# Attention over paired blocks of queries: which block of a pair goes first, the one of many keys or the one of few

## What is computed

```python
o_a = swa_prompt(qa, ka, va, mk_a, mv_a, attn_sinks, slopes_a)    # window: this chunk of 64 and the two before it, meta keys, a sink
o_b = dsa_prompt(qb, qi, wi, kb, vb, ki, mk_b, mv_b, slopes_b, n_sel_p)  # top 256 of all earlier keys, meta keys
mix = (jax.nn.sigmoid(g_a) * o_a + jax.nn.sigmoid(g_b) * o_b) @ w_o
x = x + rms_norm(mix, g_post_mix)
hid = jnp.square(jax.nn.relu(rms_norm(x, g_pre_mlp) @ w_up))
return x + rms_norm(hid @ w_down, g_post_mlp)
```

## Time and profile before

| what | value |
|---|---|
| median of 3 runs | 1979.54 us (1978.48 to 1980.01) |
| the profiled execution's own time | 1977.99 us |
| its span, first to last instruction | 1976.2 us |
| PE busy | 1888.3 us, 96% |
| DVE busy | 1158.8 us, 59% |
| mean granted clock of PE | 0.982 |
| `attention` on PE | about 582 to 1040 us of the span |

### The profile page before, as it was taken

One profiled execution on the slowest core, in us unless ns is written; L12 is line 12 of the kernel. 1 busy time (PEld: TensorE's weight loads), 2 busy tenths in 40 slices (PEclk: granted clock), 3 DMA queues, 4 the chain that ended last, 5 costly groups with the idle time before them and its releaser, 6 DMA issues. The chain is left out here.

```text
span 1976.2 us, 32638 instructions
## 1 busy us (share of the span) xinstructions
PE 1888.3 (96%) x11780; PEld 1785.9 (90%) x11780; DVE 1158.8 (59%) x2747; ACT 711.8 (36%) x1420; POOL 584.8 (30%) x445
## 2 busy tenths in 40 slices
PE   5999999999999999999997979999999999999995
PEld 5889999877779999999996859999999999999994
DVE  5249999998655666666755653333333333334436
ACT  4335544223334555555653332222222222222212
POOL 2316554234233444444311002222222222222214
PEclk9999999999998999999998989999999999999998
DMA  5423333333446444444204322111111111111204
GB/s 171 126 64 102 95 95 85 89 102 95 115 110 155 98 98 98 98 98 87 67 22 145 117 89 65 48 43 45 45 43 47 45 46 42 42 42 42 64 1 160
DMA packets 180396, 160.23 MB, mean 81 GB/s; under 512 B 101472, under 2 KB 148432, under 8 KB 180288
## 3 DMA queue, kind: packets, MB, share of 16 engines
q1 hardware_dynamic: 166144, 140.32, 25.1%
q10 hardware_dynamic: 14144, 18.49, 4.0%
HBM read 120.63 MB, written 39.27 MB: 81 GB/s over the span
## 5 line engine op out<-in xcount | busy, mean ns | idle before, releaser
L2166 PE MATMUL ps<-x2T_hi,weights 128*128 128x362 f32 (+1 forms) x1536 | 381.5, 328 | 5.3 <-DVE weights L2131 5.3
L2182 PE MATMUL ps<-hid_hi,weights 128*128 128x362 f32 (+1 forms) x1536 | 379.4, 326 | 0.0
L2166 PEld LDWEIGHTS ps<-x2T_hi,weights 128*128 128x128 f32 x1536 | 273.3, 189 | 5.5 <-DVE weights L2131 5.5
L2114 DVE TENSOR_TENSOR total<-total,ps 128x364 f32<-128x364 f32 (+1 forms) x360 | 189.2, 532 | 139.3 <-PE ps L2182 139.3
L2182 PEld LDWEIGHTS ps<-hid_hi,weights 128*128 128x128 f32 x1536 | 270.5, 188 | 0.0
L2166 PE MATMUL ps<-x2T_lo,weights 128*128 128x362 f32 (+1 forms) x768 | 252.4, 329 | 0.0
L2182 PE MATMUL ps<-hid_lo,weights 128*128 128x362 f32 (+1 forms) x768 | 250.2, 326 | 0.0
L976 PE MATMUL ps<-xT_hi,w 128*128 128x362 f32 (+1 forms) x960 | 245.1, 330 | 1.6 <-PEq L160 1.6
L2099 DVE TENSOR_TENSOR hidden<-hidden 128x362 f32<-128x362 f32 (+1 forms) x96 | 51.6, 538 | 311.0 <-ACT hidden L2072 311.0
L2032 POOL TENSOR_TENSOR weights<-down_raw,weights 128x512 fp32r<-128x512 f32 x64 | 83.0, 1296 | 391.7 <-ACT weights L2063 391.7
L951 DVE MATCH_REPLACE8 score<-top,score 128x1024 f32<-128x1024 f32 (+5 forms) x208 | 198.4, 958 | 0.0
(11 more groups left out here) (189 smaller groups left out, 3273.2 us busy)
## 6 DMA issues: line engine op xcount, KB each, us to landing
q_raw<-q_scr SPq DMA_DIRECT2D x80, 256.0 KB, 5.1
w_raw<-in_w_in ACTq DMA_DIRECT2D x64, 256.0 KB, 3.0
up_raw<-in_w_up SPq DMA_DIRECT2D x64, 256.0 KB, 2.7
down_raw<-in_w_down SPq DMA_DIRECT2D x64, 256.0 KB, 2.6
gates<-gate_scr SPq DMA_DIRECT2D x34, 256.0 KB, 4.5
x_in<-in_x_prompt SPq DMA_DIRECT2D x16, 512.0 KB, 4.8
gate_scr<-stage SPq DMA_DIRECT2D x32, 256.0 KB, 3.1
q_scr<-stage SPq DMA_DIRECT2D x40, 181.0 KB, 3.1
```

The source lines that it names most:

```text
L2114: dve.tensor_tensor(out, out, more, ALU.add).then_inc(added, 1)
L2166: last = pe.matmul(ps[:, g % UP_BANKS, 0:n], a[:, k, fs], b, start=(k == 0 and i == 0), stop=(k == KT - 1 and i == 2))
L2182: more = pe.matmul(ps[:, UP_BANKS + g % DOWN_BANKS, 0:n], a[:, f, cols], h, start=(f == 0 and i == 0), stop=(f == FT - 1 and i == 2))
```

## The change

`block_in_pair` gives the block of few keys for e = 0 and that of many for e = 1. All that is addressed by e follows: the order of quads in both branches, the place of a block's queries, its distances, its gates and results. `PAIR_DIST` is written anew, and its value is 1120 columns as before. The pairs, the tiles, the number and the shapes of all instructions are the same.

```diff
     if j == SAMPLE_TILE:
         return SAMPLE_BLOCK
-    return j if e else SAMPLE_BLOCK - 1 - j
+    return SAMPLE_BLOCK - 1 - j if e else j
...
-PAIR_DIST = dist_place(0, 1) + N_META + CHUNK
+PAIR_DIST = dist_place(0, 1) + key_columns(1, block_in_pair(0, 1))
```

## The result

| | median us | runs | ratio to before | 95% interval |
|---|---|---|---|---|
| before | 1979.01 | 18 | | |
| changed | 1982.60 | 18 | 1.0018 | 1.0012 to 1.0025 |

The changed kernel is 3.6 us slower by the medians, 0.18%. That is just within the 0.2% that the forecast called no change, and the interval reaches over it. The profiled execution took 1981.77 us, with a span of 1980.0.

A forecast was written before the change was run, and what follows sets the result against it. PE, busy 96% of the span and gapless through most of the attention, was taken as the bound. +3.5 us from section 1 and -0.3 in tile 1 gave +3.2 on 1979.54, so 1982.7 us; range 1979.7 to 1985.5.

The forecast's parts named there:

- The start of section 1: Tile 0, first score of branch B: PE arrives early and waits 2.4 us for POOL's query split, instead of 0.3.
- The quads from there: Section 1 to tile 1's second quad: S, L, S, L, A1 take 48.5 us against 45.03, so +3.5 us.
- Tiles 1 to 8: Exchanged quad neighbourhoods cost nothing where PE has no gap; -0.3 us in tile 1, 0 elsewhere, within -0.5 to +0.5.
- The split of the loss into 2.1 us of wait and the rest clock: Of the +3.5 us in section 1, 2.1 is the new wait, the rest clock; S loses 2.7 at half clock.
- The clock: Section 1 of tile 0: half clock covers the first S (6.03 us), rising near 613 in the first L (9.40).
- The late clock: Rival, chance 0.25: clock rises one or two steps later in section 1's first L; total +4.6 or +6.0 us.
- The early clock: Rival, chance 0.1: clock rises already in section 1's first S, costing 3.37, with L 8.88; total 0.0, 1979.6 us.
- The third rival: Chance 0.05: DVE sets the pace in tiles 1 to 8 and the order helps; all told -3, 1979.7 us.

The follow-up runs named there:

- e5: Changed kernel with section 0 alone taking its quads in the old order; median 1981.52 us, ratio 1.0007 to the kernel before.
- e3: Changed kernel with POOL's split of section 1's queries done in two halves, each with its own semaphore; median 1978.84 us, ratio 1.0003 to the kernel before.
- e2: Kernel before with the new order in tiles 1 to 7 only, tile 0 in the old order; median 1979.20 us, ratio 1.0004.
- e8: e7 with twenty more wide matmuls inside PE's wait for the first half of POOL's split; median 1975.56 us, ratio 0.9990 to the kernel before.
- e8b: e7b with fourteen more wide matmuls inside PE's wait for the first half of POOL's split; median 1975.65 us, ratio 0.9985 to the kernel before.
- e6r: The same kernel as e6, run again for a second profile; median 1978.29 us, ratio 1.0004 to the kernel before.
- e1: Kernel before with the new order in tile 0 only, the old one in tiles 1 to 7; median 1981.89 us, ratio 1.0017.
- e6: Changed kernel with five matmuls of 512 columns on PE ahead of section 1's wait for POOL; median 1980.10 us, ratio 0.9995 to the kernel before.
- e7: e3 with sixteen wide matmuls in PE's two idle stretches ahead of section 0; median 1978.61 us, ratio 0.9995 to the kernel before.
- e7b: Kernel before, old order, with POOL's split in halves and the wide matmuls of e7; median 1975.98 us, ratio 0.9979.

## Why the prediction was right

Forecast 1982.7, measured 1982.6. That the two lie within 0.1 is luck: the forecast added 3.2 us to a median of 3 runs, 1979.54, and 18 runs have 1979.01, so that the change forecast is +3.2 and the change measured +3.6. And in the profiled executions 0.7 to 0.8 of the difference arises behind the attention, where the forecast had nothing. The attention itself has +3.2 by X and +2.9 by Y. By its steps:

- *The start of section 1.* 2.4 us of waiting for POOL were forecast, 2.27 measured, and the first quad of section 0 took 2.40 us where "no more than the 2.94 us" stood. e5 and e3 took the wait away in two ways, one by work ahead of it and one by an earlier signal, and X fell by 2.2 and 2.6 us.
- *The quads from there.* 6.03, 9.40, 12.02, 8.88, 12.2 were forecast, 6.00, 9.35, 12.01, 8.88, 12.27 measured; +3.5 us in sum, both times. The method carried it: a quad's length depends on what is scored and on what is weighed beside it, and every new neighbourhood but one (A1 behind L) had a twin in the rows of before, and that one was built of two steps that had.
- *Tiles 1 to 8.* -0.3 was forecast for A1 behind a long quad. In the changed kernel A1 behind A14 takes 3.37 us and the lag goes from 3.38 us at 650.65 to 2.98 at the same place of tile 2. From there to the sample tile it stays between 2.96 and 3.23. e2 has the order in these tiles alone and loses nothing.
- *The split of the loss into 2.1 us of wait and the rest clock* is the weak place. The prediction puts 2.1 of its +3.5 us down to the wait and the rest, 1.4, to the clock, and then says that S loses 2.7 by the clock. 2.1 and 2.7 are 4.8: work that the wait left over is done in S at half clock, and so is in both terms. The runs give another split: 1.0 us for the work that is left behind the wait, at full clock (e8 against e8b), and 6.00 - 3.53 = 2.5 for S at half clock, together 3.5. The two are not causes that can be paid off one by one either. The wait alone is worth 2.6 (e3) and the clock alone, raised during the wait, 3.0 (e6r), more in sum than there was to lose. The total was right because it came from whole quads and not from this split.
- *The clock.* That S costs 6.0 at half clock and 3.4 at full is shown by e6r (3.16) and e8 (3.53). The rise was put near 613, 5 us after the first wide scores, and came near 611, 3 us after them. This was a miss that cost nothing: over the runs the rise came 1.8 to 5.0 us after them, and the L in which it came took 9.16 to 9.40.

**The rivals.** The late clock did not come in the changed kernel or in e1. The early clock, in S, which had 0.1, did not come without added matmuls either. In e6's profile the clock rose earlier still, in section 0, ahead of the added matmuls, and that gave nothing: PE had then only a longer wait, in which the clock fell. The third rival, help from DVE's pace, has no support: e2 gains nothing, and from 650 to 1000 us both kernels keep PE busy without a gap.

## What to carry to other kernels

Where the order of work changes but not the work, look for the places where a queue isn't full: ahead of a wait with a fixed end, finishing the first part sooner is worth nothing, and leaving more of it for afterwards costs. In a stretch at half clock the order decides what pays for it: a quad paced by VectorE at nearly no cost, a quad of narrow matmuls at nearly double. A wait of TensorE can be used: here a few wide matmuls in it whose result is not used, or a signal half-way through the work it waits for, each gave back nearly all that the order had cost. And a loss that is added up from idle time and slow clock should be checked for work that is counted in both.

## What the runs showed of the hardware

- The same section 0, with scores of 80 and 208 columns, ran at either clock. Where PE had been idle for 3.7 to 4.1 us ahead of it, the clock was at half from within 2 us of its start and stayed there to its end (0.50 from 586 to 603 in e6r, PE busy for 16.14 of 17 us), with one exception, e6. What in section 0 makes the difference (its scores, transposes or weighings) no run here took apart. Where the idle time ahead of it had been cut to about 1 us by wide matmuls, and four more of them stood in its first 2 us, the clock stayed at full through it (e7, e7b, e8, e8b).
- Five matmuls of 512 columns at half clock, 2.22 us of them from 603.76 on, had the rise while they ran: the clock was 0.50 up to 605 and 1.00 from 606 on (e6r, one profile).
- L took longer where the S whose values it weighs has a last tile of 16 keys than where it has one of 80. In the changed kernel L of 848 columns behind S of 272 (tiles of 128, 128 and 16 keys) takes 794.82 - 785.93 = 8.89 us. L of 784 columns behind S of 336 (128, 128 and 80) takes 7.53:

```profile
836.24 0.96 PE L1600 MATMUL ps<-k_b_p,q_st 128*128 128x392 f32 x4
...
843.77 0.46 PE L1600 MATMUL ps<-k_a_p,q_st 128*128 128x208 f32 x2
```

The 64 columns fewer shorten a unit's score row by 0.05 us (1.01 and 0.96), and so explain 0.2 of the 1.36 us over four units. The same pair stands in the kernel before. That the tile of 16 keys is the cause is not shown; nothing was tried on it.
